# Two-layer hybrid encoder, one core: the first loads regrouped on one queue, and a later load of the memory rows

## The reference

```
for l in range(2):
  h = rms_norm(x);  z = h @ w_in
  branch A: gelu, head norm, 128x128 spatial gate      (4 groups)
  branch B: attention with rotary, 8 query / 2 key heads
  branch M: cross-attention, 4 heads, into 256 memory tokens:
            mk, mv = split(rms_norm(mem) @ w_mem_kv[l])
  y = sum_i sigmoid(gate_i) * (branch_i @ w_br_i);  x = x + y @ w_out
  x = x + (silu(a) * b) @ w_down,   a, b = split(rms_norm(x) @ w_gate_up)
```

## Time and profile before

| what | value |
|---|---|
| median of 3 runs | 2802.2 us (2801.0 to 2802.21) |
| profiled execution, first to last instruction (span) | 2800.6 us |
| PE busy | 2772.3 us, 99% of the span |
| DVE busy | 1576.3 us, 56% |
| ACT busy | 1263.5 us, 45% |
| DMA, mean rate over the span | 191 GB/s, 535.63 MB in all |
| granted TensorE clock, mean | 0.997 of full |

### The profile page before, as it was taken

One profiled execution on the slowest core, in us unless ns is written; L12 is line 12 of the kernel. 1 busy time (PEld: TensorE's weight loads), 2 busy tenths in 40 slices (PEclk: granted clock), 3 DMA queues, 4 the chain that ended last, 5 costly groups with the idle time before them and its releaser, 6 DMA issues.

```text
span 2800.6 us, 34813 instructions
## 1 busy us (share of the span) xinstructions
PE 2772.3 (99%) x12476; PEld 2297.9 (82%) x12476; DVE 1576.3 (56%) x1771; ACT 1263.5 (45%) x1408; POOL 51.5 (2%) x74
## 2 busy tenths in 40 slices
PE   7999999999999999999999999999999999999999
PEld 5888888888888888888878888888888888888887
DVE  6676555565555455555576755555655555554554
ACT  5445444444443344344364455444444443443443
POOL 0001100000000000000000010000000000000000
PEclk9999999999999999999999999999999999999999
DMA  7544455555555555555555544555555555555553
GB/s 289 195 179 156 170 198 204 197 211 189 187 194 189 188 189 187 194 195 184 192 211 191 184 158 177 200 194 199 211 192 182 193 195 183 194 187 190 193 191 139
DMA packets 76457, 535.63 MB, mean 191 GB/s; under 512 B 8720, under 2 KB 8720, under 8 KB 13104
## 3 DMA queue, kind: packets, MB, share of 16 engines
q1 hardware_dynamic: 71776, 515.99, 51.3%
q0 software_dynamic: 4560, 17.96, 2.0%
HBM read 531.81 MB, written 2.10 MB: 191 GB/s over the span
## 4 chain that ended last, share of the span: by engine, by line
PE 96%; DVE 1%; DMA 1%; issue 1%; ACT 1%; DVEq 1%; POOL 0%; SPq 0%; ACTq 0%; POOLq 0%
PE acc L343 31%; PE acc L345 31%; PE acc L344 31%; PE tr L368 2%; DMA raw<-weights 1%; PE tr L432 1%; PE acc L400 1%; PE tr L415 0%; DVE w_lo L846 0%; DMA y<-memT_in 0%; ACT w_hi L585 0%; DVEq L971 0%; ACT b_hi L671 0%; DVEq L901 0%; ACT rows L658 0%
## 5 line engine op out<-in xcount | busy, mean ns | idle before, releaser
L846 DVE TENSOR_TENSOR w_lo<-raw,w_hi 128x1024 fp32r<-128x1024 f32 x976 | 1194.3, 1226 | 1174.4 <-ACT w_hi L585 1169.9
L585 ACT ACTIVATE w_hi<-raw 128x1024 fp32r<-128x1024 f32 x976 | 1034.6, 1061 | 1492.6 <-PE acc L345 1481.9
L343 PE MATMUL acc<-w_hi,a_hi 128*128 128x512 f32 x2560 | 1005.0, 393 | 3.0 <-issue 3.0
L345 PE MATMUL acc<-w_hi,a_lo 128*128 128x512 f32 x2560 | 996.6, 389 | 0.0
L344 PE MATMUL acc<-w_lo,a_hi 128*128 128x512 f32 x2560 | 996.3, 389 | 0.0
L344 PEld LDWEIGHTS acc<-w_lo,a_hi 128*128 128x128 f32 x2560 | 480.8, 188 | 101.9 <-issue 3.4
L345 PEld LDWEIGHTS acc<-w_hi,a_lo 128*128 128x128 f32 x2560 | 480.6, 188 | 100.3
L343 PEld LDWEIGHTS acc<-w_hi,a_hi 128*128 128x128 f32 x2560 | 480.7, 188 | 99.1 <-DVE w_lo L846 0.7
L343 PE MATMUL acc<-w_hi,b_hi 128*128 128x512 f32 x1344 | 527.3, 392 | 14.3 <-DVE b_lo L998 14.3
L344 PE MATMUL acc<-w_lo,b_hi 128*128 128x512 f32 x1344 | 524.6, 390 | 0.0
L345 PE MATMUL acc<-w_hi,b_lo 128*128 128x512 f32 x1344 | 524.4, 390 | 0.0
(11 more groups left out here) (92 smaller groups left out, 659.8 us busy)
## 6 DMA issues: line engine op xcount, KB each, us to landing
raw<-weights SPq DMA_DIRECT2D x488, 1024.0 KB, 4.8
y<-memT_in POOLq DMA_DIRECT2D x12, 512.0 KB, 7.0
bias<-bias_in POOLq DMA_DIRECT2D x24, 256.0 KB, 4.8
rows<-mem_in POOLq DMA_DIRECT2D x2, 2048.0 KB, 13.0
x<-x_in SPq DMA_DIRECT2D x1, 2048.0 KB, 18.8
out<-x SPq DMA_DIRECT2D x4, 512.0 KB, 5.0
qT<-sguT_in POOLq DMA_DIRECT2D x2, 256.0 KB, 13.1
qT<-gains_in POOLq DMA_DIRECT2D x2, 192.0 KB, 14.7
```

The lines of the kernel that those rows point to most:

```text
L343: pe.matmul(o, hi[:, kt + k, tok], wh, start=first and k == 0, stop=False)
L345: mm = pe.matmul(o, lo[:, kt + k, tok], wh, start=False, stop=last and k == HALF_KT - 1)
L585: act.activation(w_hi[:, h % SPLIT_SLOTS, :], raw[:, slot, part * HALF:(part + 1) * HALF], ACT.Copy).then_inc(hi_ready, 1)
L846: dve.tensor_tensor(w_lo[:, h % SPLIT_SLOTS, :], raw[:, slot, part * HALF:(part + 1) * HALF], w_hi[:, h % SPLIT_SLOTS, :].bitcast(F32), AL ...
```

## The change

- The semaphores and the order of the first loads: SP no longer issues `vecs_all`; it issues, with no wait between them, raw unit 0 as two halves, each followed by an eighth of `memT` (256 KB), then units 1, 2 and 3 each followed by two eighths, with `x` ahead of unit 3. POOL issues no `memT` at all.
- ACT issues `vecs_all` at its start, waits for it, and does one tiny copy from it before the layer loop.
- In each layer ACT and DVE split one half (not three) before the first operand, and one after each of the first seven operand pairs (not after the second to the sixth). ACT also waits for `second_half_loaded`.
- `take_x` for the last columns of `x` comes at s = 6, not s = 3.
- The reload of `memT` for the next layer is issued by ACT as 8 pieces, after the last `op_plain` of `y`.
- POOL issues `mem_rows` when `half_used` is 3 higher than before (`SPLIT_SLOTS + 3`); with it everything that POOL issues behind it moves.

The core of the diff:

```diff
@@ block.sync
-            sp.dma_start(vecs_all[:, :, :], vecs_in).then_inc(vecs_loaded, 16)
-            for s in range(RAW_SLOTS):
-                if s > 0:
-                    sp.wait_ge(mem_loaded[s - 1], 16)
+            def load_memory(s):
+                kt = slice(s * HALF_KT, (s + 1) * HALF_KT)
+                sp.dma_start(memT[:, kt, :], memT_in[:, kt, :]).then_inc(mem_loaded[s], 16)
+
+            sp.dma_start(raw[:, 0, 0:HALF], stream[0, :, 0:HALF]).then_inc(raw_loaded[0], 16)
+            load_memory(0)
+            sp.dma_start(raw[:, 0, HALF:], stream[0, :, HALF:]).then_inc(second_half_loaded, 16)
+            load_memory(1)
+            for s in range(1, RAW_SLOTS):
                 if s == RAW_SLOTS - 1:
                     sp.dma_start(x[:, :, :], x_in.rearrange("b (t p) d -> p (b t) d", p=P)).then_inc(x_loaded, 16)
                 sp.dma_start(raw[:, s, :], stream[s]).then_inc(raw_loaded[s], 16)
+                load_memory(2 * s)
+                load_memory(2 * s + 1)
@@ block.gpsimd
-            load_memory()
...
-                pool.wait_ge(half_used, n.at("half", SPLIT_SLOTS))
+                pool.wait_ge(half_used, n.at("half", SPLIT_SLOTS + 3))
                 pool.sem_inc(load_step, 1)
                 pool.dma_start(mem_rows, mem_in.rearrange("b (t p) d -> p (b t) d", p=P)).then_inc(memrow_loaded, 16)
...
-                pool.wait_ge(tr_done, n.at("tr"))
-                pool.sem_inc(load_step, 1)
-                load_memory()
@@ block.scalar
+            act.dma_start(vecs_all[:, :, :], vecs_in).then_inc(vecs_loaded, 16)
+            act.wait_ge(vecs_loaded, 16)
+            act.activation(stats[:, 110:111], vecs_all[:, 0, 0:1], ACT.Copy)
...
-                split(LEAD)
+                split(1)
+                act.wait_ge(second_half_loaded, 16)
                 act.wait_ge(vecs_ready, n.at("layer", 1))
-                chunk_done(LEAD)
+                chunk_done(1)
                 for s in range(FULL):
-                    if s * HALF_KT % MEM_KT == 0:
-                        act.wait_ge(mem_loaded[s * HALF_KT // MEM_KT], n.at("layer", 16, 16))
+                    act.wait_ge(mem_loaded[s], n.at("layer", 16, 16))
...
-                    if 1 <= s <= FULL - LEAD:
+                    if s < FULL - 1:
                         split(1)
...
                 op_plain(b_hi[:, 12:16, :])
+                load_memory()
                 split(1)
@@ block.vector
-                split(LEAD)
+                split(1)
...
-                    if s == 3:
+                    if s == 6:
                         dve.wait_ge(x_loaded, 16)
                         take_x(1, NC - 1).then_inc(taken[1], 1)
-                    if 1 <= s <= FULL - LEAD:
+                    if s < FULL - 1:
                         split(1)
```

More of the change, by code:

```diff
@@ L56 @@
 RAW_SLOTS = 4
-MEM_KT = KT // RAW_SLOTS
 DMA_RING = 2048
 SPLIT_SLOTS = 4
-LEAD = SPLIT_SLOTS - 1
 ACT_GROUPS = D_FF // COLS
@@ L208, in trunk @@
         sgu_done, sums_done, rs_ready = sem("sgu_done"), sem("sums_done"), sem("rs_ready")
-        mem_loaded = [sem(f"mem_loaded{s}") for s in range(RAW_SLOTS)]
+        mem_loaded = [sem(f"mem_loaded{s}") for s in range(FULL)]
+        second_half_loaded = sem("second_half_loaded")
         x_loaded, memrow_loaded = sem("x_loaded"), sem("memrow_loaded")
@@ L296, in _ @@
             pool.dma_start(rope[:, :, :, :], rope_in).then_inc(rope_loaded, 16)
-            with n.loop(DEPTH, bias=N_BRANCH * NC, head=N_HEADS, tr=TR_LAYER, half=2 * N_UNITS) as layer:
-                pool.wait_ge(half_used, n.at("half", SPLIT_SLOTS))
+            with n.loop(DEPTH, bias=N_BRANCH * NC, head=N_HEADS, half=2 * N_UNITS) as layer:
+                pool.wait_ge(half_used, n.at("half", SPLIT_SLOTS + 3))
                 pool.sem_inc(load_step, 1)
@@ L315, in _ @@
                     load_bias(k, layer)
-                n.add("tr", TR_Y)
-                pool.wait_ge(tr_done, n.at("tr"))
-                pool.sem_inc(load_step, 1)
-                load_memory()
-                n.add("tr", TR_LAYER - TR_Y)
                 n.add("half", 2 * N_UNITS)
-            for s in mem_loaded:
-                pool.wait_ge(s, 16 * (DEPTH + 1))
         @block.tensor
@@ L654, in head_out, with load_memory @@
                 n.add("oT")
+            def load_memory():
+                for s in range(FULL):
+                    kt = slice(s * HALF_KT, (s + 1) * HALF_KT)
+                    act.dma_start(memT[:, kt, :], memT_in[:, kt, :]).then_inc(mem_loaded[s], 16)
             def row_sums(src, t, out_):
                 return act.activation(mem_rows[:, t, :], src[:, t, :], ACT.Square, accum_out=out_[:, t:t + 1])
+            act.dma_start(vecs_all[:, :, :], vecs_in).then_inc(vecs_loaded, 16)
+            act.wait_ge(vecs_loaded, 16)
+            act.activation(stats[:, 110:111], vecs_all[:, 0, 0:1], ACT.Copy)
             with n.loop(DEPTH, half=2 * N_UNITS, tr=TR_LAYER, acc0=ACC_LAYER, acc1=ACC_LAYER, acc2=NC,
                         head=N_HEADS, pT=N_HEADS, oT=N_HEADS, layer=1):
-                split(LEAD)
+                split(1)
+                act.wait_ge(second_half_loaded, 16)
                 act.wait_ge(vecs_ready, n.at("layer", 1))
-                chunk_done(LEAD)
+                chunk_done(1)
                 for s in range(FULL):
-                    if s * HALF_KT % MEM_KT == 0:
-                        act.wait_ge(mem_loaded[s * HALF_KT // MEM_KT], n.at("layer", 16, 16))
+                    act.wait_ge(mem_loaded[s], n.at("layer", 16, 16))
                     for kt in range(s * HALF_KT, (s + 1) * HALF_KT):
@@ L828, in _ @@
                 n.add("layer")
+            for s in mem_loaded:
+                act.wait_ge(s, 16 * (DEPTH + 1))
         @block.vector
@@ L1256, in _ @@
             take_x(1, NC - 1).then_inc(x_final, 1)
-TR_Y = NC + 6 + NC
-TR_LAYER = TR_Y + NC + ACT_GROUPS
+TR_LAYER = 3 * NC + 6 + ACT_GROUPS
 ROWS_LAYER = 6 + NC
```

## The result

The changed kernel takes 2811.7 us (median of 6 runs, 2808.33 to 2814.99), the kernel before 2802.2. The ratio is 1.0035, with a 95% interval of 1.0024 to 1.0046: slower, by 9.5 us. The profiled execution took 2811.56 us, its span is 2809.9 us, 9.3 more than before.

A forecast was written before the change was run, and what follows sets the result against it. PE was taken as the bound, busy 2772.3 of 2800.6 us. Layer 1 (-2.8), layer 2 (+8.3) and slow clock (+4.0) sum to +9.5: profiled 2810.1, with the median's offset 2811.7, stated as 2811.5 us; range 2801 to 2816.

The forecast's parts named there:

- The chain of 12.2 us: ACT's and DVE's fixed sequence from row sums to second transposes of x, without slack: 12.2 us after mem_rows lands, both layers.
- Rival 2: Chain after mem_rows has slack, so transposes follow sooner than 12.2 us and the start's gain stays; 2793 us, chance 0.08.
- The start: Kernel start: split h0 on ACT from 6.3 us, first matmul with b_hi at about 9.7 us, 10.9 us earlier.
- The issue in layer 1: POOL waits for three more halves (h0 to h2) and issues mem_rows at 20.8 us.
- The landing: mem_rows takes 13.7 us to land in layer 1 and 13 in layer 2, beside SP's queue.
- Layer 1 to the second transposes: mem_rows at 34.5 us plus 12.2 puts them at 46.7 against 49.49: 2.8 us earlier.
- Layer 2 to the second transposes: mem_rows at 1433.8 us plus 12.2 puts them at 1446.0 against 1437.73: 8.3 us later.
- The clock: Slow clock behind PE's new stops of some 5 us at the transposes: 2.0 us each, 4.0 together.
- Priced at nothing: No cost for layer boundary, ACT's eight memT issues, fewer halves split ahead, take_x at s = 6, or second_half_loaded wait.
- Rival 1: mem_rows lands nearly undisturbed, in 7 to 11 us: -3.2 to +4.8 us, 2799 to 2807 us, chance 0.18.
- Rival 3: The start does not come 10.9 us earlier; with h0 at 14 us, +13.8, 2816 us; chance 0.1.

The follow-up runs named there:

- only3: The kernel before with only the later load of mem_rows (SPLIT_SLOTS + 3) added; 2815.86 us, ratio 1.0049 to the kernel before.
- undo3: The changed kernel with POOL's wait ahead of mem_rows back at SPLIT_SLOTS, nothing else; 2799.19 us, ratio 0.9993 to the kernel before.
- early2: The changed kernel with the later load of mem_rows in layer 1 only; 2802.12 us, ratio 1.0004 to the kernel before.
- defer: The changed kernel with POOL's small loads (sguT, gains, first bias rows) issued only when mem_rows has landed; 2812.66 us in one run.
- nocopy: The changed kernel without ACT's wait for vecs_all and its tiny copy ahead of the loop; 2812.86 us in one run.
- fewbytes: undo3 with POOL's small loads (0.98 MB) issued only when mem_rows has landed and h5 is done; 2796.51 us, ratio 0.9983 to the kernel before.
- best1: The changed kernel with mem_rows one half later in layer 1, none in layer 2, POOL's small loads behind it; 2797.27 us, ratio 0.9985 to the kernel before.
- reorder: The changed kernel with h8 to h10 and x's first op_gain ahead of the mem_rows wait, row sums and rsqrt; 2799.38 us, ratio 0.9994 to the kernel before.
- best3: best1 with x issued behind unit 3 and its two eighths on SP's queue; 2797.99 us, ratio 0.9988 to the kernel before.
- best2: The loads of best1 with the ACT and DVE order of reorder; 2799.86 us, ratio 0.9993 to the kernel before.

## Why the prediction was right, point by point

The time was right (2811.5 forecast, 2811.7 measured), and the mechanism was: only3 and undo3 show that the later load alone costs 14 and 12.5 us. The chain and the clock held. The issue and the landing in layer 1 and the landing in layer 2 were off: at the second transposes layer 1 came out 3.4 us above the forecast and layer 2 4.0 us below. That the total is right to 0.2 us is luck, since these two errors cancelled.

- **The chain of 12.2 us** held, in four kernels (before, after, early2, only3), 12.15 to 12.21 us wherever PE waited for it. Of DVE's part, `rsqrt` is 12 small operations, not 13. Rival 2 is out.
- **The start.** Forecast 9.7 us, measured 10.65. Two steps failed, and each would have given most of the miss alone. "ACT's table load happens before, at its copy": the table was loaded at 1.33 and again at 5.92, at the first activation in the loop, so split h0 began at 7.21 and not at 6.3. And "the wait for `second_half_loaded` ends before ACT gets there", priced at nothing for a landing at about 6.2 us: the second half was there only at 8.3, ACT's first operand began at 8.59, and PE 2.06 us later. In ten of the eleven kernels with the new start ACT waited there, 0.32 to 0.67 us, and in all ten the first matmul came 2.06 to 2.07 us behind that operand. In defer the half came in time and the first matmul was at 10.51. nocopy alone does not tell the two apart. The identity came earlier than forecast (zeros done at 5.9).
- **The issue in layer 1.** Forecast 20.8, measured 22.20: 0.95 from the later start, 0.3 because h0 itself took longer (10.65 to 16.17, where ACT wakes for its slot, against 20.58 to 25.78), and 0.1 from the end of h2 to POOL's issue.
- **The landing.** Forecast 13.7 and 13 us, measured 15.7 and 10.5. Both terms are mis-sized. In layer 1 the bytes were right (2.35 MB forecast, 2.36 moved), but POOL's queue moved 0.15 MB a us, where I had taken 0.19 from the stretch of before. In layer 2 I had let 2.63 MB of POOL's queue pass before the landing; from 1421.7 to 1432.2 us it moved 2.21 MB, beside 1.70 of SP's. At the forecast's 0.23 MB a us these 0.4 MB are 1.8 of the 2.5 us; the rest is SP's queue, at 0.16 MB a us and not 0.19. The direction of the correction that I made to the measured 11.3 was wrong.
- **Layer 1 to the second transposes.** Forecast 2.8 us earlier, measured 0.61 later. The issue and the landing, 1.4 and 2.0 us, are the whole difference.
- **Layer 2 to the second transposes.** Forecast 8.3 us later, measured 4.3 (33.95 less 29.61, from ACT's first operand). 2.5 us of the difference are the landing. Another 1.4 come from the layer boundary: I took its slow clock as given, and POOL's issue hung on h0, h1 and h2 running as before. Here h0 ran at full clock, and POOL issued 11.3 us behind ACT's first operand, not 12.7.
- **The clock.** Forecast 2.0 us behind each new stop. Measured from the second to the fourth transposes: 14.43 us against 12.79 in layer 1, 1.6 more, and 15.23 against 12.78 in layer 2, 2.5 more. Sum 4.1 of 4.0.
- **Priced at nothing.** ACT's eight loads of `memT` took from 597.97 to 602.3 us in the profile, 4.3 us where 3 were forecast; the next two splits ran together behind them, and PE waited for neither. Fewer halves split ahead cost nothing: in undo3 PE waits only where a transfer is late, but for 0.24 us at the second transposes. `take_x` at s = 6 held up nothing in the changed kernel. The one item of this list that failed is the wait for `second_half_loaded`, above.

Rival 1, a landing in 7 to 11 us, did not happen in layer 1, but in layer 2 the 10.5 us lie within it. With the issue at the layer's start `mem_rows` took 8.9 us there (undo3 and early2), beside only 0.64 MB of SP's. Rival 3 happened in its smallest form, 0.95 us of later start. The Trainium skill, DMA: Bandwidth & Descriptors, "Anatomy of one DMA", gives 6.8 us for such a transfer from POOL. In the 13 kernels measured here it took 8.9 to 15.7 us, so that figure was a lower bound here and no estimate beside a full queue.

One thing was not seen in the prediction, since it did not come to bear: I took the 10.9 us of the start as a gain that only `mem_rows` would give back. It isn't one. In the kernel before, the engines already moved data at 0.42 MB a us until 41 us; starting PE earlier only turns its one long stop into several short ones, and what was kept of it is 1.3 us at the fourth transposes (60.93 in undo3 against 62.28), or 3.7 to 4.0 when 0.98 MB of loads that nobody needs yet go behind (58.58 in fewbytes, 58.25 in best1).

## What to carry to other kernels

When a load is put off to leave room for others, add its landing time beside the full queue, not its time alone, to the work that stands behind its wait in program order, and see whether that sum still ends before TensorE arrives; do it for every turn of the loop, since the wait is in the loop and the crowd that it avoids is only in the first. Where the first stage moves data at the full rate from its start, an earlier start of TensorE is no gain in itself: count the bytes that must land before its last wait, and move those that may come later behind them.

## What was unexpected of the hardware

- The slow clock at the layer boundary is not the same in all executions. In each of the 13 profiles PE stopped there for 2.19 us. In nine of them, before, early2 and only3 among them, the granted clock was then at 1.2 GHz for some 3 to 4 us, and the first transposes of layer 2 came 22.7 to 22.9 us behind ACT's first operand. In four (the changed kernel, undo3, reorder, fewbytes) the clock stayed at the upper level, and they came after 21.2 us: 1.6 us less. No run shows what decides it. Elsewhere, the stops of 1.08 us (before, layer 1) and 1.78 us (undo3) were followed by no slow clock, and those of 2.09 us (defer, layer 2), 2.27 us (best3), 2.29 us (best2) and all longer ones by some of it.
- A first activation ahead of a loop does not spare the table load in it: 1.28 us at 1.33 and 1.28 us again at 5.92. Without the first one (nocopy) PE's first matmul came at the same time, 10.59 us.
- `vecs_all`, 54 KB, took 4.8 us to land on ACT's queue beside SP's first loads, and 1.9 us as SP's first load before.
